# The first expert's rows are fetched at the end of the routing stage instead of at the start of the expert stage

## The reference, cut to what matters

```python
g_p, g_idx = lax.top_k(g_prob, 1)                 # one group of 8 experts
e_p, e_idx = lax.top_k(e_prob, TOP_K)             # two experts in that group
expert_ids = g_idx * EXPERTS_PER_GROUP + e_idx
def expert_block(args):
    xb, e = args
    return (jax.nn.silu(xb @ w_gate[e]) * (xb @ w_up[e])) @ w_down[e]
y = jax.ops.segment_sum(y_buf[dest] * sw[:, None], st, num_segments=T)
```

## Time and profile before

| | us |
|---|---|
| median of 3 runs | 3375.11 |
| lowest and highest | 3374.97, 3381.01 |
| the profiled execution | 3374.41 |
| its span | 3372.6 |
| routing to experts in layer 0: last scatter issued, first gate product | 873.75, 894.29 |
| the same in layer 1 | 2838.06, 2857.58 |

### The profile page before, as it was taken

The page is one execution under the profiler, slowest core; times in us unless marked ns, Lnnn a source line. Parts: engine busy times, 40 slices in busy tenths (PEclk is TensorE's granted clock), DMA queues, the critical chain, the costliest instruction groups (busy, mean ns, idle before and its releaser), DMA issues. The chain is left out here.

```text
span 3372.6 us, 56801 instructions
## 1 busy us (share of the span) xinstructions
PE 3116.4 (92%) x19621; PEld 2476.7 (73%) x19621; DVE 1686.9 (50%) x4096; ACT 1243.0 (37%) x2675; POOL 1819.8 (54%) x1447
## 2 busy tenths in 40 slices
PE   6999999899699998899799999999998996999992
PEld 4788887688588997799565666666665885899992
DVE  3555556577444343555355556555671564444433
ACT  2444445222132332444344444444442221233223
POOL 2555555244344443344488898889885222444444
PEclk8999999999799999899799999999998997999996
DMA  3001011644699996465602211221111645999986
GB/s 105 28 28 41 30 39 58 211 154 140 229 313 314 322 318 165 130 158 151 159 10 54 51 31 36 54 51 29 39 60 63 210 150 169 311 318 313 321 246 219
DMA packets 359497, 491.69 MB, mean 146 GB/s; under 512 B 87165, under 2 KB 286609, under 8 KB 357000
## 3 DMA queue, kind: packets, MB, share of 16 engines
q1 hardware_dynamic: 325992, 412.83, 38.7%
q0 software_dynamic: 33312, 76.43, 9.0%
HBM read 362.79 MB, written 135.09 MB: 148 GB/s over the span
## 5 line engine op out<-in xcount | busy, mean ns | idle before, releaser
L2210 POOL TENSOR_TENSOR keep_wg<-keep_wg,ab_pT 128x1024 f32<-128x1024 f32 (+2 forms) x320 | 598.7, 1871 | 87.8 <-ACT ab_pT L2244 46.0
L2244 ACT ACTIVATE ab_pT<-ab_S 128x512 f32<-128x512 f32 (+4 forms) x704 | 349.8, 505 | 507.8 <-PE ab_S L2342 246.8
L2271 DVE TENSOR_REDUCE ab_mx<-ab_W 128x2 f32<-128x800 f32 (+1 forms) x224 | 249.7, 1117 | 206.6 <-PE ab_W L2356 201.9
L1352 POOL DMA_INDIRECT scratch_h<-ex_y,ex_prow x65 | 104.5, 1607 | 433.3 <-ACT ex_yr L1393 247.6
L1534 PE MATMUL ex_G<-ex_xT,keep_wg 128*128 128x160 f32 x2080 | 295.2, 300 | 0.0
L1534 PEld LDWEIGHTS ex_G<-ex_xT,keep_wg 128*128 128x128 f32 x2080 | 286.3, 191 | 0.8 <-issue 0.8
L2391 PE MATMUL ab_O<-ab_pT,keep_wg 128*64 128x512 f32 (+4 forms) x1408 | 263.0, 515 | 0.0
L350 POOL TENSOR_TENSOR aa_prob<-aa_prob,aa_rden 128x1024 f32<-128x1024 f32 x68 | 127.4, 1896 | 191.5 <-DVE aa_rden L517 191.5
L2391 PEld LDWEIGHTS ab_O<-ab_pT,keep_wg 128*64 128x64 f32 x1408 | 93.3, 139 | 145.3 <-issue 115.4
L1381 ACT ACTIVATE ex_act_g<-ex_G 128x320 f32<-128x320 f32 x65 | 28.5, 439 | 450.6 <-PE ex_U L1534 450.6
L1355 POOL DMA_INDIRECT scratch_h<-ex_yr,ex_prow x65 | 166.3, 2558 | 19.8 <-issue 19.8
(11 more groups left out here) (337 smaller groups left out, 8260.1 us busy)
## 6 DMA issues: line engine op xcount, KB each, us to landing
keep_wg<-in_moe_w_gate SPq DMA_DIRECT2D x65, 1024.0 KB, 6.9
over_hi<-in_moe_w_up SPq DMA_DIRECT2D x32, 1024.0 KB, 9.1
over_lo<-in_moe_w_down SPq DMA_DIRECT2D x32, 1024.0 KB, 10.6
over_q_hi<-in_moe_w_up SPq DMA_DIRECT2D x17, 1024.0 KB, 9.0
over_q_lo<-in_moe_w_down SPq DMA_DIRECT2D x17, 1024.0 KB, 10.9
scratch_h<-pr_h SPq DMA_DIRECT2D x33, 512.0 KB, 5.2
scratch_xn<-pr_xn SPq DMA_DIRECT2D x33, 512.0 KB, 2.9
pr_o<-scratch_oT SPq DMA_DIRECT2D x32, 512.0 KB, 4.8
```

What stands on the lines that cost most here:

```text
L2210: nc.gpsimd.tensor_tensor(to, to, pT[:, U % RING, :, 0:n], ALU.add).then_inc(added, 1)
L2244: nc.scalar.activation(pT[:, U % RING, h, 0:n], S[:, h, 0:n], ACT.Exp, scale=B_SCALE).then_inc(exped, 1)
L2271: nc.vector.reduce_max(mx[:, :, t, c:c + 1].rearrange("p h a -> p (h a)"), W[:, j % 2, :, 0:n], AX.X).then_inc(emptied, 1)
```

## The change

The two small list reads, the row numbers and the two gathers of expert 0 move from the start of the expert stage into the end of the routing stage, ahead of its barrier. Their tiles (`x`, `xr`, `slot`, `grow` of buffer 0) are allocated around both stages. The prefetch of two down matrices at the end of routing is removed; the expert stage loads all down matrices itself. In the expert stage the semaphores of expert 0's list and row numbers are raised by plain increments, and the first list read and gather issued are those of expert 1. PE waits for expert 0's rows on two semaphores that outlive the barrier. Some waits change their counts by one for buffer 0. Nothing else on any engine changes.

```diff
@@ project_and_route, SP
                 for e in range(4):
                     sp.dma_start(ups[e], ...).then_inc(keep["up_in"][e], 16)
-                for e in range(2):
-                    sp.dma_start(downs[e], io["moe_w_down"][layer, e].rearrange("(c p) f -> p c f", p=P)).then_inc(keep["down_in"][e], 16)
+                for b in range(2):
+                    sp.wait_ge(scattered[b], 32 * ((T + 1 - b) // 2))
+                sp.dma_start(keep["slot"][:, 0, :], dram["slot"][0:P, :]).then_inc(keep["slot_in"], 16)
+                sp.dma_start(keep["slot"][:, 1, :], dram["slot"][P:CAP, :].unsqueeze(0).to_broadcast([QN, REST, 2])).then_inc(keep["slot_in"], 16)
@@ project_and_route, POOL
                 for b in range(2):
                     pool.wait_ge(scattered[b], 32 * ((T + 1 - b) // 2))
+                    pool.wait_ge(xn_out[b], 16 * ((T + 1 - b) // 2))
+                pool.wait_ge(keep["sources"], layer + 1)
+                pool.sem_inc(held, 1)
+                pool.indirect_dma_start(keep["x"][:, :], None, dram["xn"],
+                                        bass.IndirectOffsetOnAxis(ap=keep["grow"][:, 0:1], axis=0)).then_inc(keep["x_in"], 16)
+                pool.indirect_dma_start(keep["xr"][:, :], None, dram["xn"].rearrange("r (j d) -> (r j) d", j=QN),
+                                        bass.IndirectOffsetOnAxis(ap=keep["grow"][:, 1:2], axis=0)).then_inc(keep["xr_in"], 16)
@@ project_and_route, DVE, after the counts
+                dve.wait_ge(keep["quarter_in"], 16)
+                dve.wait_ge(keep["slot_in"], 32 * (layer + 1))
+                nc.vector.tensor_scalar(keep["grow"][:, 1:2], keep["slot"][:, 1, 0:1], float(QN), keep["quarter"][:, :], ALU.mult, ALU.add)
+                nc.vector.tensor_copy(keep["grow"][:, 0:1], keep["slot"][:, 0, 0:1])
+                dve.drain().then_inc(keep["sources"], 1)
@@ experts, SP, step 0
-                        slots_of(e)
+                        sp.sem_inc(slot_in[0], 32)
                         slots_of(e.back(-1))
                         sp.dma_start(ident[:, :], io["ident"]).then_inc(consts, 16)
@@ experts, SP, down matrices
-                        if f.turn is None and f.c < 2:
-                            sp.wait_ge(keep["down_in"][f.c], 16 * (layer + 1))
-                            sp.sem_inc(d_in[f.slot4], 16)
-                        else:
-                            sp.dma_start(wd[f.slot4], weights_of("moe_w_down", f)).then_inc(d_in[f.slot4], 16)
+                        sp.dma_start(wd[f.slot4], weights_of("moe_w_down", f)).then_inc(d_in[f.slot4], 16)
@@ experts, POOL, step 0
-                        gather(e)
                         gather(e.back(-1))
@@ experts, DVE, step 0
-                        find_sources(e)
+                        dve.sem_inc(sources, 1)
                         find_sources(e.back(-1))
                         find_places(e)
@@ experts, PE
                 def step(e):
+                    if e.turn is None and e.c == 0:
+                        pe.wait_ge(keep["x_in"], 16 * (layer + 1))
+                        pe.wait_ge(keep["xr_in"], 16 * (layer + 1))
+                    elif e.live(N):
+                        pe.wait_ge(x_in[e.slot4], landed(e, 1))
                     if e.live(N):
-                        pe.wait_ge(x_in[e.slot4], (e.uses4 + 1) * 16)
```

More of the change, by code:

```diff
@@ L47 @@
 BEYOND = 2 * KEYS // P
+REST = CAP - P
+QN = P // REST
+QD4 = D // QN
 assert CAP > P and BEYOND == EXPERTS
@@ L1193, in experts @@
         s = Space(nc, ctx, f"ex{layer}")
-        REST = CAP - P
-        QN = P // REST
-        QD4 = D // QN
         N = EXPERTS + layer
@@ L1210, in experts @@
         wd_hi, wd_lo = s.sb("wd_hi", [P, 2, FC, D], F32R), s.sb("wd_lo", [P, 2, FC, D], F32R)
-        slot = s.sb("slot", [P, 4, 2, 2], I32)
+        slot = [keep["slot"][:, :, :]] + [s.sb(f"slot{k}", [P, 2, 2], I32)[:, :, :] for k in range(1, 4)]
         grow = s.sb("grow", [P, 4, 2], I32)
@@ L1214, in experts @@
         share = s.sb("share", [P, 8, 2])
-        x = s.sb("x", [P, 4, D])
-        xr = s.sb("xr", [P, 4, QD4])
+        x = [keep["x"][:, :]] + [s.sb(f"x{k}", [P, D])[:, :] for k in range(1, 4)]
+        xr = [keep["xr"][:, :]] + [s.sb(f"xr{k}", [P, QD4])[:, :] for k in range(1, 4)]
         xT = s.sb("xT", [P, 2, DC, CAP])
@@ L1254, in last, with landed @@
             return e.turn is None and e.c == N - 1
+        def landed(e, more):
+            return (e.uses4 + more - (1 if e.slot4 == 0 else 0)) * 16
         def pick(t, e):
@@ L1272, in slots_of @@
                         at = sp.value_load(extra[0:1, 1 + BEYOND:2 + BEYOND], min_val=0, max_val=EXPERTS * STRIDE)
-                        sp.dma_start(slot[:, e.slot4, 0, :], dram["slot"][bass.ds(at, P), :]).then_inc(slot_in[e.slot4], 16)
-                        sp.dma_start(slot[:, e.slot4, 1, :],
+                        sp.dma_start(slot[e.slot4][:, 0, :], dram["slot"][bass.ds(at, P), :]).then_inc(slot_in[e.slot4], 16)
+                        sp.dma_start(slot[e.slot4][:, 1, :],
                                      dram["slot"][bass.ds(at + P, REST), :].unsqueeze(0).to_broadcast([QN, REST, 2])).then_inc(slot_in[e.slot4], 16)
                         return
-                    sp.dma_start(slot[:, e.slot4, 0, :], pick(slots[:, 0:P, :], e)).then_inc(slot_in[e.slot4], 16)
+                    sp.dma_start(slot[e.slot4][:, 0, :], pick(slots[:, 0:P, :], e)).then_inc(slot_in[e.slot4], 16)
                     rest = pick(slots[:, P:CAP, :], e).unsqueeze(0).to_broadcast([QN, REST, 2])
-                    sp.dma_start(slot[:, e.slot4, 1, :], rest).then_inc(slot_in[e.slot4], 16)
+                    sp.dma_start(slot[e.slot4][:, 1, :], rest).then_inc(slot_in[e.slot4], 16)
                 def weights_of(name, e):
@@ L1331, in gather @@
                     pool.sem_inc(held, 1)
-                    pool.indirect_dma_start(x[:, e.slot4, :], None, dram["xn"],
+                    pool.indirect_dma_start(x[e.slot4], None, dram["xn"],
                                             bass.IndirectOffsetOnAxis(ap=grow[:, e.slot4, 0:1], axis=0)).then_inc(x_in[e.slot4], 16)
-                    pool.indirect_dma_start(xr[:, e.slot4, :], None, xn_parts,
+                    pool.indirect_dma_start(xr[e.slot4], None, xn_parts,
                                             bass.IndirectOffsetOnAxis(ap=grow[:, e.slot4, 1:2], axis=0)).then_inc(xr_in[e.slot4], 16)
@@ L1408, in find_sources @@
                     dve.wait_ge(slot_in[e.slot4], (e.uses4 + 1) * 32)
[L1409 to L1413, removed]
+                    if e.after(5):
+                        dve.wait_ge(x_in[e.slot4], landed(e, 0))
+                        dve.wait_ge(xr_in[e.slot4], landed(e, 0))
+                    nc.vector.tensor_scalar(grow[:, e.slot4, 1:2], slot[e.slot4][:, 1, 0:1], float(QN), quarter[:, :], ALU.mult, ALU.add)
+                    nc.vector.tensor_copy(grow[:, e.slot4, 0:1], slot[e.slot4][:, 0, 0:1])
                     dve.drain().then_inc(sources, 1)
                 def find_places(e):
+                    if e.turn is None and e.c == 0:
+                        dve.wait_ge(slot_in[0], 32)
                     if e.after(8):
                         dve.wait_ge(y_out[e.slot4], (e.uses4 - 1) * 32)
-                    nc.vector.tensor_scalar(prow[:, e.slot8, 1:2], slot[:, e.slot4, 1, 0:1], float(QN), quarter[:, :], ALU.mult, ALU.add)
-                    nc.vector.tensor_copy(prow[:, e.slot8, 0:1], slot[:, e.slot4, 0, 0:1])
-                    nc.vector.tensor_copy(share[:, e.slot8, :], slot[:, e.slot4, :, 1].bitcast(F32))
+                    nc.vector.tensor_scalar(prow[:, e.slot8, 1:2], slot[e.slot4][:, 1, 0:1], float(QN), quarter[:, :], ALU.mult, ALU.add)
+                    nc.vector.tensor_copy(prow[:, e.slot8, 0:1], slot[e.slot4][:, 0, 0:1])
+                    nc.vector.tensor_copy(share[:, e.slot8, :], slot[e.slot4][:, :, 1].bitcast(F32))
                     dve.drain().then_inc(listed, 1)
@@ L1521, in step @@
                             for c in range(4 * b, 4 * b + 4):
-                                last = nc.tensor.transpose(T[:, (b + e.c) % 2, P * (c % 4):P * (c % 4) + P], x[:, e.slot4, P * c:P * c + P], ident[:, :])
+                                last = nc.tensor.transpose(T[:, (b + e.c) % 2, P * (c % 4):P * (c % 4) + P], x[e.slot4][:, P * c:P * c + P], ident[:, :])
                             last.then_inc(flipped, 1)
@@ L1538, in step @@
                         pe.wait_ge(x_act, e.count(2, 1))
-                        pe.wait_ge(xr_in[e.slot4], (e.uses4 + 1) * 16)
+                        if e.turn is not None or e.c > 0:
+                            pe.wait_ge(xr_in[e.slot4], landed(e, 1))
                         for k in range(DC // QN):
-                            last = nc.tensor.transpose(T[:, e.c % 2, P * k:P * k + P], xr[:, e.slot4, P * k:P * k + P], ident[:, :])
```

(9 more changed lines are left out.)

## The result

The changed kernel takes 3385.55 us (median of 10 runs, 3381.78 to 3391.28), the kernel before 3374.62 in the same comparison. The ratio is 1.0035, 95% interval 1.0027 to 1.0043: slower by 9 to 14.5 us. Forecast were 3385.2 and slower. The sum came out right, but three of its terms did not, and they partly cancel: the barrier (forecast unchanged, cost 4.6 us), the last scatter (forecast -0.8, gave -3.3) and the contention with the down loads (forecast +2.6, cost 5.6).

The account below looks back on a forecast made before the run. PE bounds the expert stage, but time is won or lost at the boundary from routing to experts. 13.71 - 6.11 = +7.60, then +2.6 - 0.8 + 1.4 gives +10.8 us on 3374.4: 3385.2, range 3378 to 3392.

Parts of the forecast that it names:

- the barrier: Between routing and experts: clearing and meeting stay at 2.16 us in layer 0 and 1.67 in layer 1.
- the last scatter: End of routing: without the down loads the last scatter lands 0.4 us a layer sooner, -0.8, bounds 0 and -1.6.
- the contention with the down loads: Start of the expert stage: down loads beside the gather of x(1) slow it, +2.6 us, bounds 0 and 5.2.
- The first gate product waits for x(1), so a gather of x(0) ahead of the barrier saves little: Behind the barrier: PE turns x(1) before expert 0's gate product, so only 2.82 + 3.29 = 6.11 us are saved.
- The piece from list read to gather moves in front: Ahead of the barrier: this piece and two gather issues are added, 6.89 + 6.82 = 13.71 us in two layers.
- the first rival: At the barrier: POOL's DRAIN holds until the xr gather has landed, up to 7.6 us more, 3392.8; chance 0.10.
- The clock: Start of the expert stage: PE's clock rises late in both layers, as in layer 1 before, +1.4 us.
- the second rival: End of routing: without the weights the last scatter lands much sooner, no slowdown, 3377.0 or 3372.8 us; chance 0.15.

Follow-up runs that it names:

- a_down: The changed kernel with the prefetch of two down matrices back at the end of routing: 3384.6 us, ratio 1.0028 to the kernel before.
- a_late: The changed kernel with SP waiting for the gather of expert 1 to land before it issues the first down load: 3382.2 us, ratio 1.0024.
- a_lists: The changed kernel with down loads held for expert 1's gather and both expert 0 gathers back behind the barrier: 3370.1 us, ratio 0.9990.
- b_late: The kernel before without the down prefetch in routing, SP's first down load waiting for the gather of expert 1 to land: 3373.7 us, ratio 0.9995.
- b_warm: The kernel before with PE turning the identity 24 times, results unused, at the start of the expert stage: 3374.8 us, ratio 0.9994.
- b_late_warm: The kernel before with both the late down loads of b_late and the extra PE transposes of b_warm: 3370.7 us, ratio 0.9984.
- b_nodown: The kernel before without the prefetch of two down matrices in routing; the expert stage loads them itself: 3381.0 us, ratio 1.0021.
- a_ups_behind: The changed kernel with two of the four up loads issued only when the row numbers are ready, beside expert 0's gathers: 3396.3 us, ratio 1.0061.
- a_wait: The changed kernel with POOL waiting for both gathers of expert 0 to land before it enters the barrier: 3390.3 us, ratio 1.0046.

## Why the prediction was right, and where its terms were not

1. *The first gate product waits for x(1), so a gather of x(0) ahead of the barrier saves little*: right. In the changed kernel x(0) is turned at 892.91, on the arrival of the index row, and PE then waits 4.99 us for x(1).
2. *The piece from list read to gather moves in front, 4.64 and 4.57, then two issues of 2.25*: right, 4.70 and 4.66, and 2.24 (883.77 + 0.96 - 882.49) and 2.25 (2854.38 + 0.96 - 2853.09).
3. *"The barrier itself I leave at 2.16 and 1.67 us"*: wrong, and the first rival, at 0.10, had the mechanism. From the end of the xr issue to B the changed kernel takes 4.56 and 3.89 us, +2.4 and +2.2. The rival's 7.6 was too dear: xr lands 3.8 and 3.5 us after its start, not 4.4 to 5.2, and part of the barrier's old cost, the DRAIN's own 0.55 us, lies inside the wait. SP's DRAIN of 7 ns, which I held against it, was that of another kind of DMA, as I had noted.
4. *The last scatter, -0.8, bounds 0 and -1.6*: mis-sized. From S to the first event behind the landing it is 2.15 and 2.18 in place of about 3.9 and 3.7, -3.3 in all, outside the bounds. I took the scatter of 2794.48 for one in a lightly loaded stretch, but the DMA share is 0.99 from 2793 to 2795; and I read the quiet end of the wait (0.09 from 876 to 877, nothing from there to the landing at 877.65) as proof that the loads did not matter. The engines had been full until just before that, as this window of the kernel before shows:

```profile
875.00:876.00 1.00, 0.00 (x0) 0.00 (x0) 0.00 (x0) 0.00 (x0) 0.00 (x0) 0.50 0.91 354
```

   The scatter was issued at 873.75, into engines busy to 876, and landed after they had emptied. That the loads are the cause is shown by the kernels without them (2.1 us in the changed kernel) and by a_down, which puts them back (4.53 and 3.82 us to the list read). The Trainium skill's rule ("DMA: Bandwidth & Descriptors", latency and other measured facts), 0.2 us to HBM on average and 2 at high load, gave -3.6; the trace agrees with its size (-3.3). Whether memory latency or the queue is the reason no run here tells apart, but a queue would fit: in both layers before, and in layer 0 of a_down, the landing comes 1.7 to 1.8 us after the DMA share has fallen below one half.
5. *Contention with the down loads, +2.6, bounds 0 and 5.2*: the mechanism right (a_late, a_down), the size short. From B to the transposes of x(1) it cost 1.1 and 4.5 us, +5.6. The down load was forecast from about B+3 and came at B+5.09 and B+4.38, in layer 0 just behind the gather of x(1) and in layer 1 just ahead of it. The row the term was sized by, a gather deep in the expert stage, does not show that case.
6. *The clock, +1.4*: from the transposes of x(1) to the up products layer 0 takes 7.02 us in place of 6.23 and layer 1 7.25 in place of 7.62, +0.4.

Terms 3 to 6 by the rows: +4.6 -3.3 +5.6 +0.4 = +7.3, where the prediction had -0.8 +2.6 +1.4 = +3.2. With points 1 and 2 (+7.7) that is the profiled execution's +15, against a forecast of +10.8; the median lies 4 us below that execution, near the forecast. So the agreement of the medians to 0.4 us is luck: errors of both signs in the terms, and a gap between profile and median that nothing here explains. The sign was not luck. It rests on points 1 and 2, a net 7.6 us that the relief of the last scatter would have had to give back; that mechanism, the second rival's, was real but gave back 3.3, and the first rival's worked the other way.

The medians rank as the profile's sums do, with one exception: a_lists, by its sum (-2.5) behind b_late, b_warm and b_late_warm, has the lowest median of all. It was timed apart from those three; by the ratios it comes second, behind b_late_warm, and the intervals overlap. b_late_warm and a_lists are the two that beat the kernel before beyond their intervals; between those two the timing does not decide.

## What to carry to other kernels

Work moved ahead of a barrier is on the path up to that barrier: move it only if the barrier's last arrival comes later anyway, and ask whether the first consumer behind it needs this item or the next one. Look at what an engine has in flight when it enters a barrier: issuing a GpSimd gather "without waiting" right ahead of one was a wait for its landing. A prefetch on the same DMA engines cost whoever stood beside it: at the end of routing the last scatter, at the start of the expert stage the first gathers. Held until those had landed it cost least by the profile. The timing shows that against loading at once in the kernel before (b_late 3373.7, b_nodown 3381.0), and not against the prefetch in routing.

## What the runs showed of the hardware

- GpSimd's DRAIN at the barrier held until the indirect DMAs that it had issued had landed, ending 0.3 to 0.4 us after: 5.14 and 4.85 us in the changed kernel, 8.32 and 8.48 in a_ups_behind, and 0.55 with nothing in flight (before, a_lists). These records begin up to 2 us before the last gather's issue is over. SyncE's DRAIN took 0.14 and 0.16 us right behind its list reads.
- An indirect scatter of 1 KB (128 rows of 8 bytes) landed 2.1 us after issue with idle DMA engines, and 3.7 to 4.5 behind 1 MB loads (before, a_down).
- The rows of a 512 KB gather were used 4.2 to 4.5 us after its issue with no 1 MB load beside it (a_late), 4.7 with one issued 1.0 us behind it (b_nodown), 6.4 to 7.7 with one 0.2 to 0.7 us behind it (changed, a_wait, a_ups_behind, b_nodown), and 8.8 with one 0.4 us ahead of it (the same without b_nodown).
- Transposes whose results nobody uses brought the granted clock from 0.50 to 1.00 while PE would have stood still (b_warm); from the first gate product to the first up product it then took 4.35 and 4.34 us, where the kernel before took 4.50 and 5.86.
